# Turns inside the mixer's inverse levels as 64x64 products on array quarters, and second products staggered behind the next pair's first product

## What is computed

```python
def _rwkv7_step(S, inp):
    r_t, w_t, k_t, v_t, kk_t, a_t = inp
    sa = jnp.einsum('bshvk,bshk->bshv', S, -kk_t)
    S = S * w_t[..., None, :] + sa[..., None] * (kk_t * a_t)[..., None, :] + v_t[..., None] * k_t[..., None, :]
    y = jnp.einsum('bshvk,bshk->bshv', S, r_t)
    return S, y
```

## Time and profile before

| | us |
|---|---|
| median of 3 runs | 1177.79 |
| lowest and highest | 1177.7 and 1181.29 |
| span of the profiled execution | 1173.6 |
| the six stretches of levels, first L955 to first L994, sum | 150.9 |

### The profile page before, as it was taken

One profiled execution on the slowest core, in us unless ns is written; L12 is line 12 of the kernel. 1 busy time (PEld: TensorE's weight loads), 2 busy tenths in 40 slices (PEclk: granted clock), 3 DMA queues, 4 the chain that ended last, 5 costly groups with the idle time before them and its releaser, 6 DMA issues. The chain is left out here.

```text
span 1173.6 us, 28618 instructions
## 1 busy us (share of the span) xinstructions
PE 997.6 (85%) x12572; PEld 609.4 (52%) x12572; DVE 502.5 (43%) x1378; ACT 316.8 (27%) x733; POOL 96.0 (8%) x128
## 2 busy tenths in 40 slices
PE   3899998778788999999856999879878999999930
PEld 3866666567675465333315655557766465333310
DVE  0103855352625335433116248655566444433226
ACT  1231116332332032212113411355433032212110
POOL 1200000000100000132110000000010000121110
PEclk9899998997899989999987999899989999999975
DMA  9977726243537536899955323200010654899851
GB/s 350 310 216 260 246 92 244 81 154 138 200 135 194 203 130 228 304 390 372 358 188 155 135 95 89 72 3 4 4 46 10 244 180 176 305 383 379 319 205 54
DMA packets 144568, 224.44 MB, mean 191 GB/s; under 512 B 20700, under 2 KB 98761, under 8 KB 143616
## 3 DMA queue, kind: packets, MB, share of 16 engines
q1 hardware_dynamic: 131712, 185.61, 46.4%
q0 software_dynamic: 10592, 29.64, 6.9%
q10 hardware_dynamic: 2128, 7.21, 1.6%
HBM read 216.73 MB, written 21.14 MB: 203 GB/s over the span
## 5 line engine op out<-in xcount | busy, mean ns | idle before, releaser
L1534 ACT ACTIVATE region<-bank 128x512 f32<-128x512 f32 (+3 forms) x322 | 155.1, 512 | 241.7 <-PE bank L1441 73.8
L1415 PE MATMUL bank<-region 128*32 128x512 f32 x1152 | 171.3, 600 | 9.1 <-issue 6.5
L1415 PEld LDWEIGHTS bank<-region 128*32 128x32 f32 x1152 | 48.4, 111 | 112.2 <-issue 112.2
L1153 PE MATMUL bank<-u,ring 128*128 128x384 f32 x320 | 106.5, 488 | 0.0
L1319 PE MATMUL bank<-ring,u 128*128 128x512 f32 x192 | 89.5, 624 | 8.1 <-DVE u L2285 5.9
L1441 PE MATMUL bank<-ring,region 128*32 128x512 f32 x768 | 87.3, 595 | 1.4 <-ACT region L1534 1.4
L1153 PEld LDWEIGHTS bank<-u,ring 128*128 128x128 f32 x320 | 59.9, 190 | 40.5 <-issue 1.4
L2203 DVE COPY_PREDICATED region<-lev,bank 128x256 f32<-128x256 uint8 x90 | 34.4, 443 | 105.4 <-PE bank L976 105.4
L1601 ACT ACTIVATE region<-bank 128x384 f32<-128x384 f32 x50 | 23.7, 492 | 168.7 <-PE bank L1153 96.7
L1319 PEld LDWEIGHTS bank<-ring,u 128*128 128x128 f32 x192 | 37.7, 199 | 54.9 <-issue 44.9
L2418 DVE TENSOR_TENSOR region<-region,bank 128x256 f32<-128x256 f32 x24 | 10.1, 422 | 124.6 <-ACT region L1846 95.7
(11 more groups left out here) (298 smaller groups left out, 1508.6 us busy)
## 6 DMA issues: line engine op xcount, KB each, us to landing
ring<-in_w_mod SPq DMA_DIRECT2D x48, 1024.0 KB
region<-in_moe_w SPq DMA_DIRECT2D x48, 1024.0 KB
ring<-in_moe_w SPq DMA_DIRECT2D x48, 1024.0 KB
ring<-in_w_in SPq DMA_DIRECT2D x20, 768.0 KB
region<-y_rows SPq DMA_DIRECT2D x6, 1024.0 KB, 7.7
region<-g_rows POOLq DMA_DIRECT2D x4, 1024.0 KB, 6.6
ring<-in_w_in SPq DMA_DIRECT2D x12, 256.0 KB
ring<-in_w_out SPq DMA_DIRECT2D x4, 768.0 KB
```

What stands on the lines that cost most here:

```text
L1153: last = pe.matmul(dst[:, 0:T], w[:, c, tc(m)], u[:, c, :], start=(c == 0), stop=(c == KT - 1))
L1415: last = pe.matmul(bank[p % 2][cols, :], xs[:, p % 2, c, cols], of[(p * P + CTILE * q) // CAP][:, c, :], start=(c == 0), stop=(c == KT - 1))
L1534: return act.activation(dst, src, ACT.Copy)
```

## The change

The two 128x128 transposes of a turn become eight ordinary 64x64 products of a matrix of `xx_m` (as the stationary operand) with `half_ident`, each on one array quarter, in the order of the first product: d, then e, then p. Since a quarter can write to any bank, the turned matrices stand in the banks by chunk `p` and no longer by direction `d`: `ut_m[:, j, 4 * p + 2 + d]` in place of `4 * d + 2 + p`, which the second product now reads. Columns, banks, the copy and the masked copy are the same. The second product of a pair moves up: it is issued behind the next pair's first product and turn, and that of the last pair (j = 2) behind pair 0's first product and turn of the next level. The last level's third second product stands alone behind its loop. `tok` and `masked` stay behind the level's loop, now with one second product fewer ahead of the next level. Only TensorE's program changes.

```diff
--- before.py
+++ after.py
@@ -943,40 +943,53 @@
 
                 tok(0)
                 tok(1)
+                def first_product(k, j):
+
+                    if k == 1:
+                        pe.wait_ge(at_up, NJ * (n + 1))
+                    else:
+                        pe.wait_ge(x_up, lev_step(l, s, k - 1, j))
+                    for d in range(2):
+                        for e in range(2):
+                            for p in range(2):
+                                pe.matmul(bank[2 * j + p][rows64(e), d * C:(d + 1) * C],
+                                          at_m[rows64(p), j, 2 * d + e, :], xx_m[rows64(p), j, 2 * d + e, :],
+                                          start=True, stop=True)
+                    if l + 1 < DEPTH and j == 1 and k >= 2:
+                        mod_turn(l + 1, 4 * s + k - 2, 2 * P, bank[3])
+                    if l + 1 < DEPTH and j == 2 and k <= 4:
+                        mod_rows(l + 1, 4 * s + k - 1, bank[5][:, tc(2)])
+                    for d in range(2):
+                        for e in range(2):
+                            for p in range(2):
+                                last = pe.matmul(bank[2 * j + p][rows64(e), (2 + d) * C:(3 + d) * C],
+                                                 xx_m[rows64(p), j, 2 * d + e, :], half_ident[rows64(p), :], start=True, stop=True)
+                    last.then_inc(t_mm, 1)
+
+                def second_product(k, j):
+
+                    pe.wait_ge(t_cp, lev_step(l, s, k, j))
+                    for d in range(2):
+                        for e in range(2):
+                            for p in range(2):
+                                last = pe.matmul(bank[2 * j + e][rows64(p), d * C:(d + 1) * C],
+                                                 ut_m[rows64(e), j, 4 * p + 2 + d, :], ut_m[rows64(e), j, 4 * p + d, :],
+                                                 start=True, stop=True)
+                    last.then_inc(x_mm, 1)
+
                 for k in range(1, LEVELS):
-                    for j in range(NJ):
-                        if k == 1:
-                            pe.wait_ge(at_up, NJ * (n + 1))
-                        else:
-                            pe.wait_ge(x_up, lev_step(l, s, k - 1, j))
-                        for d in range(2):
-                            for e in range(2):
-                                for p in range(2):
-                                    pe.matmul(bank[2 * j + p][rows64(e), d * C:(d + 1) * C],
-                                              at_m[rows64(p), j, 2 * d + e, :], xx_m[rows64(p), j, 2 * d + e, :],
-                                              start=True, stop=True)
-                        if l + 1 < DEPTH and j == 1 and k >= 2:
-                            mod_turn(l + 1, 4 * s + k - 2, 2 * P, bank[3])
-                        if l + 1 < DEPTH and j == 2 and k <= 4:
-                            mod_rows(l + 1, 4 * s + k - 1, bank[5][:, tc(2)])
-                        for d in range(2):
-                            last = pe.transpose(bank[2 * j + d][:, tc(1)], xx_m[:, j, 2 * d:2 * d + 2, :].rearrange("p e n -> p (e n)"),
-                                                ident)
-                        last.then_inc(t_mm, 1)
+                    first_product(k, 0)
+                    if k > 1:
+                        second_product(k - 1, NJ - 1)
+                    for j in range(1, NJ):
+                        first_product(k, j)
+                        second_product(k, j - 1)
                     if k == 1:
                         tok(2)
                         tok(3)
                     if 2 <= k < 2 + NJ:
                         masked(k - 2)
-                    for j in range(NJ):
-                        pe.wait_ge(t_cp, lev_step(l, s, k, j))
-                        for d in range(2):
-                            for e in range(2):
-                                for p in range(2):
-                                    last = pe.matmul(bank[2 * j + e][rows64(p), d * C:(d + 1) * C],
-                                                     ut_m[rows64(e), j, 4 * d + 2 + p, :], ut_m[rows64(e), j, 4 * p + d, :],
-                                                     start=True, stop=True)
-                        last.then_inc(x_mm, 1)
+                second_product(LEVELS - 1, NJ - 1)
 
                 if l + 1 < DEPTH:
                     pe.wait_ge(modt_cp, N_MOD * (l + 1) + 4 * (s + 1))
```

## The result

The change made the kernel slower: 1191.66 us median (1185.95 to 1194.56, 4 runs) against 1177.74 (1172.78 to 1181.29, 4 runs), a ratio of 1.0136 with a 95% interval of 1.0093 to 1.0179. I had forecast 1161.8 with a range of 1155 to 1172. The profiled execution is the shortest of the four, span 1183.4 us against 1173.6.

What follows compares the result with a forecast made beforehand. TensorE's own program was taken to bound the levels. Savings of 11.4 us in layer 1 and 7.5 in layer 0, less 0.9 and 2 given back, made 16.0 us: 1161.8 us, range 1155 to 1172.

Steps and rivals of the forecast that it cites:

- Group 0.25: In the levels, a group of 8 products (16 records) on TensorE was priced at 0.25 us.
- Turn after 0.25: A pair's turn as eight quarter products was priced at 0.25 us, for 0.51 before, saving 0.26.
- The rival of 0.50: Turns run at the pace of `values`, 0.50 us each, costing as much as before: 1181 us, chance 0.07.
- The levels' plan: Order and timing in layer 1's levels with `masked`: 3.99 us becomes 3.05, saving 0.94 in each of levels 2 to 4.
- a wait of 0.22: TensorE's wait at a level's end, ahead of the next level's first product, was to vanish, saving 0.22 us.
- the planned 3.05: Forecast length in us of a layer 1 level with `masked`, for 3.99 before.
- What is given back: Losses set against the savings: 0.9 us behind the levels in step 1, and 2 us for late instructions.
- the plan had 18.9: Forecast saving in the six stretches of levels: 11.4 us in layer 1 and 7.5 in layer 0.
- The rival had it: Instruction fetch becomes the bound in the levels; with packets every 3.4 us the kernel is slower, 1194 us, chance 0.06.
- What is given back in step 1: In both layers the way on starts from ScalarE's third copy, losing 0.45 us of a step's saving, 0.9 in two.
- The clock did not do it: Rival: clock falls of about 4 us each, or more stops, eat half the gain: 8 saved, 1169.8 us, chance 0.13.
- The rule on transpose mode: Float32 transposes are 4× faster than products; taken alone, a turn of some 1 us and a kernel some 40 us slower.

Runs made afterwards that it cites:

- e8: Only the second products staggered, turns left as 128x128 transposes, against the kernel before, run a second time: 1168.89 us, ratio 0.9958 (0.9934 to 0.9983).

## Why the prediction was wrong, point by point

- **The prices of the array held.** Group 0.25: 0.23 to 0.25. Turn after 0.25: 0.23; it does not run like `values`. The rival of 0.50 fell. The reason that I gave for `values` was not needed: in its code the rows and the columns of a product are both `rows`, so its products lie on two of the four quarters, and half the quarters could by itself make 31 ns a record of 13 to 16. No run separates this from both halves writing one bank.
- **The levels' plan held for the order.** I had a wait of 0.22 gone and `x_up` in time; e8 shows levels of 3.65 us without waits. The one level with `masked` of the changed kernel that met only a short stop (layer 1, step 2, level 2) took 3.44 us, about 0.3 of it in that stop, for the planned 3.05.
- **The step that failed is in "What is given back": "I charge 2 us, one more such stop, with ends of 0 and 6."** I treated late instructions as accidents beside weight traffic, to be counted. The experiments show a rate, at best 256 instructions in 3.47 us in layer 1 once the store is used up. Stops of over 0.3 us inside the stretches were 5.2 us before, all in layer 0 (1.3, 1.7, 2.2), and are 35.6 us now: 19.1 in layer 0 (6.0, 4.9, 8.2) and 16.5 in layer 1 (6.0, 6.0, 4.6), where there had been none. That is 30.4 us against a charge of 2. Outside these stops the stretches fell from 148.0 to 135.2 us, 12.8 where the plan had 18.9.
- **The rival had it, at a chance of 0.06.** "If the next could come only every 2.9 us or later" the change loses, and at 3.4 us the kernel would be at 1194; measured were 3.47 us and 1191.7. That the two times are so near is in part luck, since the rival's sum left out what happens between the stretches. What I held against it was a misreading of the earlier trace rows: 1.0 us is how long a packet occupies a DMA engine, not how soon the next one follows. The same row also says one packet per 4 us while TensorE took 62 instructions per us, 84% of the 74 that turned out to be the limit. The kernel before stood just under it, and in its trace 384 records never passed in less than 11.02 us, 70 instructions per us. A rate that a change nearly doubles and that no row shows should have had a chance near that of the forecast.
- **What is given back in step 1** (0.9 us) could not be seen beside stops of this size.
- **The clock did not do it.** The granted clock was 0.933 over the profiled execution of the changed kernel and 0.925 before, and 0.97 to 1.00 in layer 1's levels.
- **The rule on transpose mode**, which the prediction cites from the Trainium skill (TensorE: Matmul & The Clock Gate, section Terms), pointed to a slower kernel, and that came true for another reason. Taken alone it gave a turn of some 1 us; the turn took 0.23. What cost was the count: one float32 product is two records and, with its weight loads, four instructions, where a transpose is one record and two instructions, so eight products are 32 instructions for 4.
- **The total is smaller than the sum of the stretches.** They lost 17.6 us; the medians differ by 13.9 and the profiled spans by 9.8 (the median lies 8.3 us above the profiled span now, for the 4.2 that I had kept). Between the two mixers, where both programs are the same, the profiled execution took 428.9 us for 436.3. In the other kernels that part varied from 429.2 to 437.2, so I take it for the spread between executions; no run isolates it.

**Still open.** That a stop ends with the arrival of a packet rests on the count of 128 records, on the 3.47 us and on one packet per interval. That instructions are held in store is inferred from the levels that ran faster than that at the start of a step; how many they are, and what sets the 2.4 us between the transfer and the restart, is not shown. How much weight traffic lengthens the interval in layer 0, where single stops reach 3.0 us, was not tried apart.

## What to carry to other kernels

Count TensorE's instructions per microsecond as well as its array time: a float32 product costs four, and here 74 per us, 256 in 3.47 us, was the most that layer 1 got from one stop to the next. Short stretches ran faster (the changed kernel passed 384 records in 8.74 us), but 768 records never took less than 19.59 us in any run, 78 per us. So a long stream of 64x64 float32 products ran at about half the pace of the array. An edit that replaces one large operation by many small ones is worth its array time only where the new rate stays below that limit. In the trace of before the limit showed as packets per microsecond, as the nearest dense stretch, and as a few stops a multiple of 128 records apart. Beside the limit, look for array time that costs no instructions: an order that fills waits gave 0.4 to 0.6%, and with operations of one tile shape grouped as well it was 1.0%.

## What the runs showed that I had not expected

- Instructions come to TensorE in packets of 256, in layer 1 at best one in 3.47 us; often the interval is 3.74 or 3.75 instead.
- A 64x64 float32 product with 8 moving columns is nearly as dear as one with 64: 16 full records last 0.28 us until the next group starts, 16 of 8 columns 0.30, in which one change to 128x128 is included.
- Products of 64 rows by 128 columns of weights have a long cost of their own: 8 records in 0.66 us, 272 ns each at the median, and a turn of about 0.7 us.
